# A table of PSUM banks in the lru part, mod_b tiles one place later, and the attention reciprocal in two halves

## The chip, the cores and the metric
The kernel runs on one core of a Trainium2 chip. The metric is the device time of one execution in microseconds (us); before the change three runs gave 1354.24, 1352.58 and 1350.67 us, so the median is 1352.58 us.

## What is computed
Two transformer-like blocks on one sequence of 512 tokens with 1024 channels, all in fp32. Cut to what matters:

```python
# first block
p = modulate(rms(x), shift1, scale1) @ w_in          # q, kv, k_pe, f, ga, gb
q, k, v = mla(p); attn = softmax(q k^T) v            # 8 heads, 512 + 256 keys
x = x + g1 * ((sigmoid(ga)*(attn@w_o) + sigmoid(gb)*(fft2(f)@w_f)) @ w_out)
x = x + g2 * expert_choice(modulate(rms(x), shift2, scale2))    # 16 experts
# second block
z = rms(x) @ w_in_2                                  # lru_x, lru_gate, sc_b, sc_c, sc_x
u = causal_conv4(lru_x)
h = linear_recurrence(u, gates r and i of u)         # y_lru = h * gelu(lru_gate)
y_sc = sc_b * causal_conv3(sc_c * sc_x)
x = x + concat(y_lru, y_sc) @ w_out_2
x = x + (gelu(conv3(h2@w_g)) * conv3(h2@w_u)) @ w_down
return rms(x)
```

The vectors shift1, scale1, g1, shift2, scale2, g2 are the modulation: `silu(c) @ w_mod + b_mod`.

## The kernel before
**Products.** Activations lie with channels on the partitions, so a tile is 128 channels by 512 tokens and fills one PSUM bank. A weight block is 128x128. Each fp32 product is made from three fp32r ones (`mm3`, L958 to L960): high part by high part, high by low, low by high. A projection of 1024 channels takes 8 blocks of three matmuls, 24 in all, for one tile (`project`).

**Weights.** SyncE loads chunks of 1 MB (16 blocks) into a ring of four raw buffers. ScalarE copies each to the high part (`w_hi`, L1702) and GpSimd subtracts it for the low part (`w_lo`, L892), into rings of three. ScalarE does so in its own program order, once the chunk that had the place is used up (`SPLIT_DUE`).

**Order and banks.** `make_plan` lists every PSUM tile in TensorE's order, gives each a bank (by a table, or round robin over the banks of a `phase`), and notes which semaphore frees it. `open_tile` (on TensorE) waits until the tile that had the bank before is freed. Nobody else decides the order: every engine has one program written out by hand, and what stands behind a waiting instruction waits with it.

**mod_b.** The last two thirds of the modulation are not done by TensorE's array but by VectorE: `modulation_b(c)` multiplies and adds eight slices of a raw chunk (L2108, L2110) and leaves a column sum `macc`; TensorE only adds its partitions (`mod_b_tile`, L995: four matmuls of one column), and VectorE reads the result (`mod_b_evac`, L2095). There are 16 of these. TensorE has them behind the tiles of ga, gb and four_o: number 0 stands behind ga tile 3, number 5+j behind gb tile j, number 12+j behind four_o tile j for j = 1 to 3. VectorE gets to `modulation_b(0)` only when it is done with the q rows (`q_rows`, L2292 the add of the rotated part). Number c+4 is made behind the evacuation of number c, and the raw chunks of weights stand in the same ring behind those of mod_b.

**Attention.** For each head h, TensorE makes six score tiles (`sT`), with the maxima of the next head between them (`max_pair`, L1237), then `pv` (L1271), the transposed maxima, and the transposes of q and k of head h+2. On VectorE, each head is: `head_lo(h+1)`, three ops (L2354) that give the low parts of q and k of the next head and so free banks 5, 3 and 4 for its score maxima; `maxima(h+1)` (L2363); `head_output(h-1)` (L2373, one operand in PSUM). In every even head from 2 on, `pair_output` follows: the reciprocal of the pair's sums `rs` (L2380, 128x512) and the product `att*rs` (L2381, both operands in SBUF). GpSimd adds up the probabilities of each head (`add_probs`, L915) and, after heads 1, 3 and 5, makes one `w_lo` (L892).

**lru part.** TensorE makes the eight lru_x tiles, behind them pairs of small gate tiles (lru_r, lru_i, L1535 and L1538) from the convolved channels `conv_u` (VectorE, L2626 to L2637, `lru_conv`), then for four groups sc_c, sc_x, sc_b, then eight lru_gate tiles, then mix_o (`w_out_2`; the first two tiles together, block by block, over four y_sc and eight y_lru parts). An lru_x tile is freed by `conv_done`, lru_r by ScalarE, lru_i by `lru_b_done` (VectorE, L2642), lru_gate by the low part of y_lru (L2073). The first two lru_x tiles have banks 3 and 4; from the third on banks go round robin over eight in the order 0, 1, 2, 5, 6, 7, 3, 4, and so to the end of lru_gate. By this, lru_x 5 has the bank of lru_x 3, lru_gate 6 and 7 have banks 0 and 1, and mix_o has

```python
bank=(0, 1, 2, 3, 4, 5, 4, 5)[j]
```

so that mix_o 0 and 1 take the banks of lru_gate 6 and 7.

Of the kernel before, what the change touches and what calls it, by code (L numbers as in the profile page):

```python
# [19 lines left out]
H = 8  # L20
# [13 lines left out]
LRU = 8  # L34
# [16 lines left out]
B = 128  # L51
# [4 lines left out]
FH = T // 2  # L56
# [19 lines left out]
def q_block(half, k):  # L76

    i = half * QL + k
    return S1_Q + i // 5 * CH + i % 5 * QW
# [123 lines left out]
def blocks(base, first, count, width=B):  # L203

    return range(base + first // CH, base + (first + count * width - 1) // CH + 1)


def split_steps():

    o = Order()  # L210
    for j in range(KD):
        o.add("h", j)
    for j in range(KD):
        o.add("hc", j)
    o.add("f", 0)
    o.add("f", 1)
    for j in range(QL):
        o.add("cq", j)
    for j in range(KL):
        o.add("ckv", j)  # L220
    o.add("f", 2)
    o.add("f", 3)
    for g in range(NF + 1):
        if g < NF:
            o.add("f_ch", g, 0)
            o.add("f_ch", g, 1)
        if g >= 1:
            o.add("four", g - 1)
    for h in range(H):
        o.add("q", h)  # L230
        o.add("k", h, 0)
        o.add("k", h, 1)
    for j in range(4):
        o.add("attn", j)
    for j in range(KD):
        o.add("m", j)
    for i in range(PAIRS):
        o.add("ye", i, 0)
        o.add("ye", i, 1)
    for j in range(KD):  # L240
        o.add("g", j)
    for j in range(SC):
        o.add("y_sc", j)
    for j in range(LRU):
        o.add("y_lru", j)
    for j in range(KD):
        o.add("g2", j)
    for q in range(QUARTERS):
        for i in range(FQ):
            o.add("ff", q, i)  # L250
    return o


SPLITS = split_steps()
# [7 lines left out]
PRE_FF = PRE_SC + SC + LRU  # L262
GATES_AFTER = {3: (0,), 4: (1, 2), 5: (3,), 6: (4,), 7: (5,)}
GATES_LAST = (6, 7)


SQ0 = 5 + QL + KL + 1
# [10 lines left out]
def make_plan():  # L278
    p = Plan()
# [37 lines left out]
    for half in range(2):  # L317
        for t in range(TT):
            p.add("uq", half, t, by=("qtok_done", half * TT + t + 1), bank=half * TT + t,
                  split=[c for k in range(QL) for c in blocks(s1, q_block(half, k), 1, QW)])  # L320
    p.phase(6)
    for j in range(KD):
        p.add("ga", j, by="act", split=blocks(s1, S1_GA + j * 8 * B, 8))
        if j >= 3:
            p.add("mod_b", j - 3, by=("modb_done", j - 2))
    for j in range(KD):
        p.add("gb", j, by="act", split=blocks(s1, S1_GB + j * 8 * B, 8))
        p.add("mod_b", 5 + j, by=("modb_done", 6 + j))

    def four_o(j, bank=None):  # L330
        p.add("four_o", j, by=("resid_done", j + 1), split=blocks(s1, S1_FO[j], NF), bank=bank)

    for j in range(KD // 2):
        four_o(j)
        if j >= 1:
            p.add("mod_b", 12 + j, by=("modb_done", 13 + j))
    for t in range(KT):
        p.add("uk", t, by=("ktok_done", t + 1), split=blocks(s1, S1_K, 8), bank=t)
    for t in range(KT):
# [80 lines left out]
    w = SPLIT0["w_in_2"]  # L420

    def lru_gates(i):
        p.add("lru_r", i, by="act")
        p.add("lru_i", i, by=("lru_b_done", i + 1))

    for j in range(LRU):
        if j == 2:
            p.phase(8, (0, 1, 2, 5, 6, 7, 3, 4))
        p.add("lru_x", j, by=("conv_done", j + 1), split=blocks(w, j * 8 * B, 8), bank=3 + j if j < 2 else None)
        for i in GATES_AFTER.get(j, ()):  # L430
            lru_gates(i)
    for j in range(SC):
        p.add("sc_c", j, split=blocks(w, (LRU + 3 * j) * 8 * B, 8))
        if j == 0:
            for i in GATES_LAST:
                lru_gates(i)
        p.add("sc_x", j, split=blocks(w, (LRU + 3 * j + 1) * 8 * B, 8))
        p.add("sc_b", j, by=("lo_done", SPLITS["y_sc", j] + 1), split=blocks(w, (LRU + 3 * j + 2) * 8 * B, 8))
    for j in range(LRU):
        p.add("lru_gate", j, by=("lo_done", SPLITS["y_lru", j] + 1), split=blocks(w, (LRU + 3 * SC + j) * 8 * B, 8))  # L440
    for j in range(KD):
        p.add("mix_o", j, by=("resid_done", RES2 + j + 1), split=blocks(SPLIT0["w_out_2"], j * 12 * B, 12),
              bank=(0, 1, 2, 3, 4, 5, 4, 5)[j])
    w = SPLIT0["ffn"]
    p.phase(5)
    for q in range(QUARTERS):
# [6 lines left out]


PLAN = make_plan()
TILE = PLAN.tiles
LAST = PLAN.last_user
# [28 lines left out]
def build(nc, stream, cols_d, x_d, ctx_d, router_d, wab_d, rope_d, rope_t_d, rot_d, dftc_d, ident_d, iota_d, xt_d, out):  # L486
    with ExitStack() as ctx:
        base = 16512

        def at(name, kb, shape, dt=F32):  # L490
            return nc.alloc_sbuf_tensor_at(name, shape, dt, offset=base + int(kb * 1024))

        def sem(name):
            return ctx.enter_context(nc.semaphore(name))
# [91 lines left out]
        rs = at("rs", R + 98, [P, T])  # L586
# [57 lines left out]
        sc_c = at("sc_c", R + 112, [P, T])  # L644
# [33 lines left out]
        freed_act = sem("freed_act")  # L678
        freed_dve = sem("freed_dve")
        hi_done = sem("hi_done")  # L680
        lo_done = sem("lo_done")
# [5 lines left out]
        modb_done = sem("modb_done")  # L687
# [48 lines left out]
        conv_done = sem("conv_done")  # L736
        a_sq_done = sem("a_sq_done")
        lru_b_done = sem("lru_b_done")
# [189 lines left out]
        def _(pe):  # L928
# [3 lines left out]
            def open_tile(*name):  # L932

                t = TILE[name]
                prev = PLAN.prev[t]
                if prev is not None:
                    pe.wait_ge(freeing[PLAN.freed[prev][0]], PLAN.freed_count(prev))
                return psum[:, PLAN.bank[t], :]
# [51 lines left out]
            def mod_b_tile(k):  # L990

                o = open_tile("mod_b", k)
                pe.wait_ge(macc_done, k + 1)
                for m in range(2):
                    last = mm(o[:, m:m + 1], macc[:, k % 4, m, :], one, start=True, stop=True)  # L995
                done(last)
# [182 lines left out]

            for j in range(KD):  # L1180
                done(project(open_tile("ga", j), s1, S1_GA + j * 8 * B, B, ks, hx))
                if j >= 3:
                    mod_b_tile(j - 3)
            for j in range(KD):
                done(project(open_tile("gb", j), s1, S1_GB + j * 8 * B, B, ks, hx))
                mod_b_tile(5 + j)
            pe.wait_ge(lo_done, SPLITS["four", NF - 1] + 1)

            def four_out(j, behind=None):
# [8 lines left out]

            for j in range(KD // 2):
                four_out(j)  # L1200
                if j >= 1:
                    mod_b_tile(12 + j)

            def token_rows(o, t, off):
                tok = slice(t * P, t * P + P)
# [365 lines left out]
            for j in range(SC):  # L1571
                for i, name in enumerate(("sc_c", "sc_x", "sc_b")):
                    done(project(open_tile(name, j), w2, (LRU + 3 * j + i) * 8 * B, B, ks, bx))
                    if i == 0 and j == 0:
                        for g in GATES_LAST:
                            gates(g)
# [108 lines left out]
        def _(act):  # L1685
# [313 lines left out]
            for j in range(SC):  # L1999
                split_weights(TILE["sc_c", j])  # L2000
                if j == 0:
                    for i in GATES_LAST:
                        lru_gates(i)
# [54 lines left out]
        def _(dve):  # L2058
            V = nc.vector
            n = [0]  # L2060

            def link(ins):

                n[0] += 1
                ins.then_inc(dve_seq, 1)
                dve.wait_ge(dve_seq, n[0])
# [26 lines left out]
            def mod_b_evac(k):  # L2093
                m = 16 + 2 * k
                V.tensor_tensor(mod[:, m:m + 2, 0], take("mod_b", k)[:, 0:2], col("b_mod", m, 2), ALU.add)\  # L2095
                    .then_inc(modb_done, 1)
# [89 lines left out]
            sums = [0]  # L2186
# [19 lines left out]
            for s in range(2):  # L2206
                w = slice(0, T) if s == 0 else slice(T, TK)
# [48 lines left out]
            for i in range(2):  # L2256
                w = rope_t[:, i * TT:(i + 1) * TT, :]
# [45 lines left out]
            for c in range(5):  # L2303
                mod_b_evac(c)
                modulation_b(c + 4)
            for c in range(5, 13):
                mod_b_evac(c)
                if c + 4 < 16:
                    modulation_b(c + 4)
# [6 lines left out]

            for j in range(KD // 2):
                four_gate(j)
                if j >= 1:
                    mod_b_evac(12 + j)  # L2320

            V.memset(k_hi[0][QK:QK + 1, :].bitcast(F32), 1.0)
            V.memset(k_lo[0][QK:QK + 1, :].bitcast(F32), 0.0)
# [45 lines left out]
            def head_output(h):  # L2369

                dve.wait_ge(o_raw, h + 1)
                r0 = (h % 2) * VD
                V.tensor_tensor(att[r0:r0 + VD, h // 2, :], psum[r0:r0 + VD, 6 + h % 2, :], att[r0:r0 + VD, h // 2, :],  # L2373
                                ALU.add).then_inc(o_sum, 1)

            def pair_output(j):

                dve.wait_ge(freed_act, PLAN.freed_count(TILE["sums", j]))
                dve.wait_ge(o_sum, 2 * j + 2)
                link(V.reciprocal(rs[:], rs[:]))  # L2380
                V.tensor_tensor(att[:, j, :], att[:, j, :], rs[:], ALU.mult).then_inc(att_done, 1)  # L2381

            def gate_behind(q):
# [10 lines left out]
            for h in range(H):  # L2394
                if h + 1 < H:
                    head_lo(h + 1)
                    maxima(h + 1)
                if h >= 1:
                    head_output(h - 1)
                if h >= 2 and h % 2 == 0:  # L2400
                    pair_output(h // 2 - 1)
            for j in range(3):
                lo(att_lo[:, j, :], att[:, j, :], att_hi[:, j, :], "attn", j).then_inc(lo_done, 1)
            head_output(H - 1)
            pair_output(H // 2 - 1)


# [169 lines left out]
            for i in range(PAIRS):  # L2577
# [24 lines left out]
                for half in range(2):  # L2602
# [5 lines left out]
                    w = slice(half * T, half * T + T)  # L2608
# [93 lines left out]
            for q in range(QUARTERS):  # L2702
                for i in range(FQ + 1):
                    if i < FQ:
# [14 lines left out]
                        if g >= 2:  # L2719
                            p = SPLITS["ff", (g - 2) // FQ, (g - 2) % FQ]  # L2720
# [14 lines left out]
            for n in range(1, len(Y_TILES), 2):  # L2735
                half, t = Y_TILES[n]
# [157 lines left out]
```

## Time and profile before

| what | value |
| --- | --- |
| median of 3 runs | 1352.58 us |
| the profiled execution, its own time | 1351.49 us |
| its span on the core | 1349.6 us |
| TensorE busy | 1319.4 us, 98% |
| VectorE busy | 691.6 us, 51% |
| ScalarE busy | 461.7 us, 34% |
| GpSimd busy | 433.2 us, 32% |
| granted TensorE clock, mean | 0.991 of full speed |

The span is the time from the first to the last instruction of the core; the execution's own time is 1.9 us longer. All rows have times from the span's start. In a timeline a row gives start, busy time, engine, line, operation, output and inputs with their shapes, a count, and in brackets the idle time of the engine just before and what ended it. The ends of matmuls overlap, so TensorE's pace is read from one start to the next.

### The profile page before, as it was taken

How to read it: one execution, taken by the hardware profiler on the slowest of the kernel's cores; microseconds unless marked ns; L12 is line 12 of the kernel's file. 1: busy time of each engine (PE TensorE's matmuls, PEld its weight loads, DVE VectorE, ACT ScalarE, POOL GpSimd, SP SyncE). 2: the span in 40 equal slices, each digit the busy share in tenths (PEclk: the TensorE clock that was granted, in tenths of full speed). 3: DMA queues.
4: the chain of work that ended last, by engine and by line, in shares of the span. 5: the costliest groups of instructions: out<-in, count | busy, mean ns of one | idle time of the engine just before them, and what ended most of it. 6: DMA issues, size and time to landing. Idle time of an engine off the chain costs nothing.

```text
span 1349.6 us, 15820 instructions
## 1 busy us (share of the span) xinstructions
PE 1319.4 (98%) x6366; PEld 970.1 (72%) x6366; DVE 691.6 (51%) x1261; ACT 461.7 (34%) x618; POOL 433.2 (32%) x136
## 2 busy tenths in 40 slices
PE   8999999999999899999999999899999999999998
PEld 5689788865578734444356788688888888888887
DVE  2465987567783723333257656512463451551553
ACT  4334222346631211121144571423342341431431
POOL 3144244237712000000024343524254345344440
PEclk9999999999999899999999999999999999999999
DMA  9521297301025899999973122223132222223101
GB/s 373 212 94 63 77 346 296 122 1 63 32 94 187 297 381 420 421 420 421 421 318 125 63 93 95 94 72 107 69 115 105 95 94 95 92 93 125 63 1 63
DMA packets 34501, 226.70 MB, mean 168 GB/s; under 512 B 4064, under 2 KB 4704, under 8 KB 8448
## 3 DMA queue, kind: packets, MB, share of 16 engines
q1 hardware_dynamic: 32992, 218.93, 42.3%
q0 software_dynamic: 1152, 4.19, 0.8%
q10 hardware_dynamic: 288, 2.62, 0.5%
q8 instruction: 48, 0.79, 0.2%
q14 instruction: 21, 0.17, 0.0%
HBM read 221.53 MB, written 4.19 MB: 167 GB/s over the span
## 4 chain that ended last, share of the span: by engine, by line
PE 91%; DVE 5%; ACT 1%; issue 1%; DMA 1%; POOL 0%; SPq 0%; DVEq 0%; ACTq 0%
PE psum L958 23%; PE psum L960 22%; PE psum L959 22%; PE psum L1463 12%; PE psum L1271 1%; PE psum L1237 1%; PE psum L1448 1%; PE psum L1451 1%; DVE q_tok L2292 1%; DMA x<-in_x 1%; PE psum L1423 1%; PE psum L1005 1%; PE psum L1672 1%; DVE rs L2380 0%; PE psum L1010 0%
## 5 line engine op out<-in xcount | busy, mean ns | idle before, releaser
L892 POOL TENSOR_TENSOR w_lo<-raw,w_hi 128x2048 fp32r<-128x2048 f32 x79 | 364.9, 4621 | 606.7 <-ACT w_hi L1702 606.7
L958 PE MATMUL psum<-b_hi,w_hi 128*128 128x512 f32 x608 | 238.7, 393 | 2.7 <-DVE conv_u L2637 2.5
L959 PE MATMUL psum<-b_lo,w_hi 128*128 128x512 f32 x608 | 237.3, 390 | 0.0
L960 PE MATMUL psum<-b_hi,w_lo 128*128 128x512 f32 x608 | 237.3, 390 | 0.0
L1702 ACT ACTIVATE w_hi<-raw 128x2048 fp32r<-128x2048 f32 x80 | 152.5, 1907 | 138.4 <-PE psum L960 105.6
L958 PEld LDWEIGHTS psum<-b_hi,w_hi 128*128 128x128 f32 x608 | 114.6, 188 | 33.6 <-issue 4.9
L960 PEld LDWEIGHTS psum<-b_hi,w_lo 128*128 128x128 f32 x608 | 114.6, 188 | 23.9
L959 PEld LDWEIGHTS psum<-b_lo,w_hi 128*128 128x128 f32 x608 | 114.4, 188 | 23.4
L1463 PE MATMUL psum<-ex_ring,xe 128*64 128x512 f32 x488 | 108.8, 595 | 0.9 <-ACT xe L1927 0.9
L2428 DVE TENSOR_TENSOR x<-psum,x 128x512 f32<-128x512 f32 x40 | 27.5, 691 | 132.2 <-PE psum L960 132.1
L958 PE MATMUL psum<-h_hi,w_hi 128*128 128x512 f32 (+1 forms) x208 | 85.2, 410 | 1.3 <-POOL w_lo L875 1.3
L960 PE MATMUL psum<-h_hi,w_lo 128*128 128x512 f32 (+1 forms) x208 | 82.7, 398 | 0.0
L959 PE MATMUL psum<-h_lo,w_hi 128*128 128x512 f32 (+1 forms) x208 | 82.4, 396 | 0.0
L1463 PEld LDWEIGHTS psum<-ex_ring,xe 128*64 128x64 f32 x488 | 34.1, 137 | 66.3 <-issue 65.4
L958 PE MATMUL psum<-ff_hi,w_hi 128*128 128x512 f32 x192 | 74.7, 389 | 0.0
L959 PE MATMUL psum<-ff_lo,w_hi 128*128 128x512 f32 x192 | 74.7, 389 | 0.0
L960 PE MATMUL psum<-ff_hi,w_lo 128*128 128x512 f32 x192 | 74.7, 389 | 0.0
L2709 DVE TENSOR_TENSOR psum<-psum,rstd_s 128x512 f32<-128x512 f32 x48 | 33.5, 697 | 77.4 <-PE psum L960 77.4
L902 POOL DMA_INDIRECT xg<-xt,ids x8 | 8.2, 1031 | 189.6 <-DVE ids L2538 138.8
L2430 DVE SCALAR_TENSOR_TENSOR x<-psum,mod,x 128x512 f32<-128x512 f32 x72 | 51.0, 743 | 25.7 <-PE psum L960 21.0
L1927 ACT ACTIVATE xe<-psum,mod,small 128x128 f32<-128x128 f32 x64 | 23.8, 458 | 83.6 <-PE psum L1423 83.6
L1463 PE MATMUL psum<-ex_ring,act_e 128*64 128x512 f32 x224 | 49.7, 595 | 0.7 <-DVE act_e L2596 0.7
(419 smaller groups left out, 2296.6 us busy)
## 6 DMA issues: line engine op xcount, KB each, us to landing
raw<-in_stream SPq DMA_DIRECT2D x97, 1024.0 KB, 4.9
ex_ring<-in_stream SPq DMA_DIRECT2D x89, 1024.0 KB, 17.3
mod_in<-in_stream SPq DMA_DIRECT2D x8, 1024.0 KB, 20.9
ex_last<-in_stream SPq DMA_DIRECT2D x7, 1024.0 KB, 17.0
x<-in_x SPq DMA_DIRECT2D x4, 512.0 KB, 6.9
x<-in_x ACTq DMA_DIRECT2D x1, 2048.0 KB, 7.4
xt<-h2t SPq DMA_DIRECT2D x8, 256.0 KB, 11.7
out<-y_out SPq DMA_DIRECT2D x8, 256.0 KB, 3.3
```

The costliest lines, as they stand in the source:

```text
L892: nc.gpsimd.tensor_tensor(w_lo[:, slot, :], raw[:, raw_slot, :], w_hi[:, slot, :].bitcast(F32), ALU.subtract).then_inc(w_lo_done, 1)
L958: mm(o, w[0], x[0], start=start, stop=False)
L959: mm(o, w[0], x[1], start=False, stop=False)
L960: return mm(o, w[1], x[0], start=False, stop=stop)
L1005: mm(psum[:, bank, 0:P], ones[:], ones[:], start=True, stop=True)
L1237: done(mm(o[:, 0:KH], q_hi[b][0:QK, q * P:(q + 1) * P], k_hi[b][0:QK, s * KH:(s + 1) * KH], start=True, stop=True))
L1463: last = mm(o[e * CAP:(e + 1) * CAP, :], x_of(k, e), w[:, (2 * (k - k0) + e) * T:(2 * (k - k0) + e + 1) * T], start=k == 0, stop=k == ks - 1)
L1702: A(w_hi[:, c % NHL, :], raw[:, n % NRAW, :], ACT.Copy).then_inc(w_hi_done, 1)
L1927: ins = A(xe[:, i % 2, k, :], o[:, j * P:(j + 1) * P], ACT.Identity, bias=mod[:, 3 * KD + k, 0:1], scale=a2[:, k:k + 1])
L2428: ins = V.tensor_tensor(x1[:, j, :], o, x1[:, j, :], ALU.add)
L2430: ins = V.scalar_tensor_tensor(out=x1[:, j, :], in0=o, scalar=scale, in1=x1[:, j, :], op0=ALU.mult, op1=ALU.add)
L2709: V.tensor_tensor(o, o, rstd, ALU.mult).then_inc(ffz_done, 1)
```

## The change
It has three parts.

**1. mod_b.** TensorE makes mod_b tile 0 behind ga tile 4 and not behind ga tile 3, and every later one is one place later too: 4+j behind gb tile j, 12+j behind four_o tile j, now from j = 0. VectorE's evacuation of tile 12 moves behind the gate of four_o 0. The round robin over six banks of this phase shifts with them.

**2. Banks of the lru part.** Tables give the banks of lru_x, lru_r and lru_i. sc_c, sc_x and sc_b of group 0 get banks 4, 5, 6; from sc_c 1 on there is a round robin over six banks. mix_o gets another table.

**3. Reciprocal.** `pair_output` no longer makes it. A new function `sums_inverse(j, half)` takes the reciprocal of one half of the 512 columns; half 0 stands at the end of the even head, half 1 at the end of the odd head after it, and `pair_output` (now only the product) behind half 1. For the last pair both halves come one after the other.

```diff
+X_BANKS = (3, 4, 0, 1, 6, 0, 1, 6)
+R_BANKS = (2, 2, 3, 2, 2, 2, 2, 3)
+I_BANKS = (5, 7, 4, 3, 5, 7, 0, 1)
...
-        if j >= 3:
-            p.add("mod_b", j - 3, by=("modb_done", j - 2))
+        if j >= 4:
+            p.add("mod_b", j - 4, by=("modb_done", j - 3))
...
-        p.add("mod_b", 5 + j, by=("modb_done", 6 + j))
+        p.add("mod_b", 4 + j, by=("modb_done", 5 + j))
...
     for j in range(KD // 2):
         four_o(j)
-        if j >= 1:
-            p.add("mod_b", 12 + j, by=("modb_done", 13 + j))
+        p.add("mod_b", 12 + j, by=("modb_done", 13 + j))
...
     def lru_gates(i):
-        p.add("lru_r", i, by="act")
-        p.add("lru_i", i, by=("lru_b_done", i + 1))
+        p.add("lru_r", i, by="act", bank=R_BANKS[i])
+        p.add("lru_i", i, by=("lru_b_done", i + 1), bank=I_BANKS[i])
 
     for j in range(LRU):
-        if j == 2:
-            p.phase(8, (0, 1, 2, 5, 6, 7, 3, 4))
-        p.add("lru_x", j, ..., bank=3 + j if j < 2 else None)
+        p.add("lru_x", j, ..., bank=X_BANKS[j])
...
     for j in range(SC):
-        p.add("sc_c", j, ...)
+        if j == 1:
+            p.phase(6, (2, 0, 3, 1, 4, 5))
+        p.add("sc_c", j, ..., bank=4 if j == 0 else None)
...
-        p.add("sc_x", j, ...)
-        p.add("sc_b", j, ...)
+        p.add("sc_x", j, ..., bank=5 if j == 0 else None)
+        p.add("sc_b", j, ..., bank=6 if j == 0 else None)
...
-              bank=(0, 1, 2, 3, 4, 5, 4, 5)[j])
+              bank=(5, 2, 0, 3, 1, 4, 1, 4)[j])
...
             for j in range(KD // 2):
                 four_out(j)
-                if j >= 1:
-                    mod_b_tile(12 + j)
+                mod_b_tile(12 + j)
...
+            def sums_inverse(j, half):
+
+                if half == 0:
+                    dve.wait_ge(freed_act, PLAN.freed_count(TILE["sums", j]))
+                w = slice(half * FH, half * FH + FH)
+                link(V.reciprocal(rs[:, w], rs[:, w]))
+
             def pair_output(j):
 
-                dve.wait_ge(freed_act, PLAN.freed_count(TILE["sums", j]))
                 dve.wait_ge(o_sum, 2 * j + 2)
-                link(V.reciprocal(rs[:], rs[:]))
                 V.tensor_tensor(att[:, j, :], att[:, j, :], rs[:], ALU.mult).then_inc(att_done, 1)
...
                 if h >= 2 and h % 2 == 0:
+                    sums_inverse(h // 2 - 1, 0)
+                if h >= 3 and h % 2 == 1:
+                    sums_inverse(h // 2 - 1, 1)
                     pair_output(h // 2 - 1)
             for j in range(3):
                 lo(att_lo[:, j, :], att[:, j, :], att_hi[:, j, :], "attn", j).then_inc(lo_done, 1)
             head_output(H - 1)
+            for half in range(2):
+                sums_inverse(H // 2 - 1, half)
             pair_output(H // 2 - 1)
```

## Rows read from the trace of the kernel before

**Rows 1.** The page's first part: busy time, share of span, instructions.
```profile
PE 1319.4 (98%) x6366; PEld 970.1 (72%) x6366; DVE 691.6 (51%) x1261; ACT 461.7 (34%) x618; POOL 433.2 (32%) x136
```

**Rows 2.** TensorE's waits: who for whom, us in total, times, longest.
```profile
PE psum L958 <- DVE ylru_lo L2073: 4.8, 1, 4.8
PE psum L995 <- DVE macc L2110: 3.0, 1, 3.0
PE psum L958 <- DVE conv_u L2637: 2.5, 1, 2.5
...
PE psum L1237 <- DVE k_lo L2354: 1.3, 2, 0.7
```

**Rows 3.** Timeline of TensorE around the wait for macc.
```profile
163.47 0.58 PE L995 MATMUL psum<-ones,macc 128*128 128x1 f32 x4 [2.95 <-DVE macc L2110]
...
168.56 0.39 PE L959 MATMUL psum<-h_lo,w_hi 128*128 128x512 f32 x1
...
171.08 0.50 PE L995 MATMUL psum<-ones,macc 128*128 128x1 f32 x4
```

**Rows 4.** Stretches: TensorE busy (x), weight loads busy (x), clock, DMA share, GB/s.
```profile
166.00:168.00 2.00, 2.00 (x6) 0.50 1.04 426
464.00:466.00 2.00, 2.00 (x11) 0.50 0.00 0
```

**Rows 5.** Timeline of TensorE, lru part, around the wait for conv_u.
```profile
734.86 0.60 PE L958 MATMUL psum<-b_hi,w_hi 128*128 128x512 f32 x1 [2.50 <-DVE conv_u L2637]
...
738.61 0.39 PE L958 MATMUL psum<-b_hi,w_hi 128*128 128x512 f32 x1
```

**Rows 6.** Timeline of TensorE, the first mix_o products.
```profile
872.53 0.76 PE L958 MATMUL psum<-ysc_hi,w_hi 128*128 128x512 f32 x1 [4.75 <-DVE ylru_lo L2073]
...
878.57 0.40 PE L960 MATMUL psum<-ysc_hi,w_lo 128*128 128x512 f32 x1
```

**Rows 7.** Timeline of GpSimd: the low part of weight chunk 11.
```profile
176.68 4.61 POOL L892 TENSOR_TENSOR w_lo<-raw,w_hi 128x2048 fp32r<-128x2048 f32 x1 [19.88 <-ACT w_hi L1702]
```

**Rows 8.** Timeline of VectorE: low part of y_lru 0, then that of y_lru 7.
```profile
849.97 0.69 DVE L2073 TENSOR_TENSOR ylru_lo<-psum,ylru_hi 128x512 fp32r<-128x512 f32 x1 [0.66 <-ACT ylru_hi L1712]
...
871.73 0.69 DVE L2073 TENSOR_TENSOR ylru_lo<-psum,ylru_hi 128x512 fp32r<-128x512 f32 x1 [0.66 <-ACT ylru_hi L1712]
```

**Rows 9.** Timeline of TensorE, heads 1 to 3: pv (L1271), first maxima (L1237).
```profile
300.77 1.94 PE L1271 MATMUL psum<-probs,v 128*64 128x512 f32 x8
...
308.19 0.62 PE L1237 MATMUL psum<-k_hi,q_hi 96*128 96x384 f32 x2
...
312.55 1.94 PE L1271 MATMUL psum<-probs,v 128*64 128x512 f32 x8
...
319.84 0.84 PE L1237 MATMUL psum<-k_hi,q_hi 96*128 96x384 f32 x2 [0.66 <-DVE k_lo L2354]
...
324.21 1.94 PE L1271 MATMUL psum<-probs,v 128*64 128x512 f32 x8
```

**Rows 10.** Timeline of VectorE, heads 2 to 4.
```profile
314.26 3.35 DVE L2380 RECIPROCAL rs<-rs 128x512 f32<-128x512 f32 x1
...
318.38 0.75 DVE L2354 SCALAR_TENSOR_TENSOR q_lo<-psum,cols,q_hi 96x512 fp32r<-96x512 f32 x1
...
325.15 0.67 DVE L2373 TENSOR_TENSOR att<-psum,att 64x512 f32<-64x512 f32 x1
328.04 0.75 DVE L2354 SCALAR_TENSOR_TENSOR q_lo<-psum,cols,q_hi 96x512 fp32r<-96x512 f32 x1 [2.21 <-ACT q_hi L1712]
```

**Rows 11.** Timeline of GpSimd: low part of a weight chunk, end of head 3.
```profile
326.84 4.58 POOL L892 TENSOR_TENSOR w_lo<-raw,w_hi 128x2048 fp32r<-128x2048 f32 x1
```

**Rows 12.** Timelines of GpSimd and VectorE, same stretch, in the attn_o stage.
```profile
389.49 4.65 POOL L892 TENSOR_TENSOR w_lo<-raw,w_hi 128x2048 fp32r<-128x2048 f32 x1 [18.63 <-ACT w_hi L1702]
...
390.50 4.19 DVE L2420 TENSOR_TENSOR m_tmp<-m_tmp,gbf 128x512 f32<-128x512 f32 x1
```

**Rows 13.** Timeline of TensorE: the shorter wait before the experts.
```profile
459.98 0.42 PE L1398 MATMUL psum<-ident,work 16*128 16x16 f32 x4 [1.78 <-DVE work L2511]
```

More of the change, by code:

```diff
@@ L422, in lru_gates @@
     def lru_gates(i):
-        p.add("lru_r", i, by="act")
-        p.add("lru_i", i, by=("lru_b_done", i + 1))
+        p.add("lru_r", i, by="act", bank=R_BANKS[i])
+        p.add("lru_i", i, by=("lru_b_done", i + 1), bank=I_BANKS[i])
     for j in range(LRU):
-        if j == 2:
-            p.phase(8, (0, 1, 2, 5, 6, 7, 3, 4))
-        p.add("lru_x", j, by=("conv_done", j + 1), split=blocks(w, j * 8 * B, 8), bank=3 + j if j < 2 else None)
+        p.add("lru_x", j, by=("conv_done", j + 1), split=blocks(w, j * 8 * B, 8), bank=X_BANKS[j])
         for i in GATES_AFTER.get(j, ()):
@@ L432, in make_plan @@
     for j in range(SC):
-        p.add("sc_c", j, split=blocks(w, (LRU + 3 * j) * 8 * B, 8))
+        if j == 1:
+            p.phase(6, (2, 0, 3, 1, 4, 5))
+        p.add("sc_c", j, split=blocks(w, (LRU + 3 * j) * 8 * B, 8), bank=4 if j == 0 else None)
         if j == 0:
@@ L436, in make_plan @@
                 lru_gates(i)
-        p.add("sc_x", j, split=blocks(w, (LRU + 3 * j + 1) * 8 * B, 8))
-        p.add("sc_b", j, by=("lo_done", SPLITS["y_sc", j] + 1), split=blocks(w, (LRU + 3 * j + 2) * 8 * B, 8))
+        p.add("sc_x", j, split=blocks(w, (LRU + 3 * j + 1) * 8 * B, 8), bank=5 if j == 0 else None)
+        p.add("sc_b", j, by=("lo_done", SPLITS["y_sc", j] + 1), split=blocks(w, (LRU + 3 * j + 2) * 8 * B, 8),
+              bank=6 if j == 0 else None)
     for j in range(LRU):
@@ L1181, in _ @@
                 done(project(open_tile("ga", j), s1, S1_GA + j * 8 * B, B, ks, hx))
-                if j >= 3:
-                    mod_b_tile(j - 3)
+                if j >= 4:
+                    mod_b_tile(j - 4)
             for j in range(KD):
                 done(project(open_tile("gb", j), s1, S1_GB + j * 8 * B, B, ks, hx))
-                mod_b_tile(5 + j)
+                mod_b_tile(4 + j)
             pe.wait_ge(lo_done, SPLITS["four", NF - 1] + 1)
@@ L2305, in _ @@
                 modulation_b(c + 4)
-            for c in range(5, 13):
+            for c in range(5, 12):
                 mod_b_evac(c)
@@ L2318, in _ @@
                 four_gate(j)
-                if j >= 1:
-                    mod_b_evac(12 + j)
+                mod_b_evac(12 + j)
             V.memset(k_hi[0][QK:QK + 1, :].bitcast(F32), 1.0)
```

## Prediction, made before the changed kernel was run
> **What bounds the kernel now.** I read the page's busy times first. TensorE is busy for 98% of the span, the others for about half or less [rows 1]: a change can gain only where TensorE stands still or runs slowly. So the list of TensorE's waits comes next. Its three largest entries are 4.8, 3.0 and 2.5 us, once each, and one of 1.3 us in two pieces comes from the attention [rows 2]. Third, the timeline around each: when TensorE resumes, its matmuls start 0.43 us apart for a while and not 0.23, and the granted clock of such a stretch is 0.50, that is 1.2 and not 2.4 GHz [rows 4]. A wait of 2.5 us or more thus costs more than itself. The pace at full clock is (171.08 - 168.56) / 11 = 0.229 us per matmul [rows 3].
>
> **Part 1, mod_b.** The same 16 tiles are made, the same DVE work is done; only TensorE's place for them moves. Before, TensorE is at tile 0 at 163.47 - 2.95 = 160.5 and waits until the column sum is there [rows 3]. With another ga tile first it gets there at 160.5 + 24 x 0.229 = 166.0, 2.5 us after the sum. The wait of 2.95 goes. From 163.47 to 171.08 lie one mod_b tile (some 0.4) and 24 matmuls (5.5): 7.6 where 5.9 is the full pace, so 1.7 of slow clock goes too. **Gain 4.65 us.** What is late next: weight chunk 11 hangs on mod_b chunks that VectorE frees, not on TensorE, so it doesn't come earlier. Its low part is done at 176.68 + 4.61 = 181.3 [rows 7]. TensorE wants it behind the 15th matmul of ga tile 7: 160.5, three whole tiles (5.5 each), three mod_b tiles (0.4 each) and 15 x 0.229 come to 181.6. The margin is 0.3 us. I count nothing, and up to 1 us for the range. After that VectorE makes a sum in 8 ops of about 0.5 us, 4.1 in all, and TensorE wants one per 5.9 us; the wait list has no second wait at L995 [rows 2]. VectorE's evacuations stand at most one place behind, where it has slack. Round robin over six banks leaves the same six tiles between users: nothing.
>
> **Part 2, banks of the lru part.** No instruction is added. lru_x 5 had the bank of lru_x 3 and waited for that tile's convolution. Now it has the bank of lru_x 2, whose convolution is one turn of VectorE (some 4 us) earlier, so the wait of 2.50 goes. The nine matmuls from 734.86 to 738.61 took 3.75, at full pace 2.06 [rows 5]: 1.7 more. **Gain 4.2 us.** lru_x 6 now needs lru_x 3 and lru_x 7 needs lru_x 4, both convolved before TensorE is there; gate tiles of ScalarE alternate on banks 2 and 3 with a whole tile between them.
>
> At the end, mix_o 0 and 1 are opened together, and mix_o 1 had the bank of lru_gate 7. So not one of their 72 matmuls could start before y_lru 7, although that is needed only as the last of twelve parts. With banks 5 and 2 they follow lru_gate 2 and 3. The wait of 4.75 goes. From 872.53 to 878.57 lie 14 matmuls: 6.04, at full pace 3.21, so 2.8 more [rows 6]. **Gain 7.6 us.** Next late is y_lru 7 itself, done at 871.73 + 0.69 = 872.4 [rows 8]; TensorE wants it 66 matmuls after 867.8, at 882.9. Margin 10 us. The six-bank round makes lru_gate 6 wait for y_lru 0, done at 849.97 + 0.69 = 850.7 [rows 8]; TensorE wants the bank two tiles before its stop at 867.8, at 856.8. Margin 6 us. VectorE, ScalarE and GpSimd are driven by TensorE's tiles there, so all of this moves forward together with the 4.2 us.
>
> **Part 3, the reciprocal.** Its cost in columns is the same: 3.35 us for 512 [rows 10], so I estimate 1.7 for each half.
>
> Good side: in head 2 the reciprocal and the product stand before head_lo(4). It starts at 318.38, and the first maxima 1.46 later, 0.66 late [rows 9, 10]. With half a reciprocal and no product VectorE is free 2.4 us earlier, which is more than the 0.66. The same in head 4 to 5. **Gain 1.3 us**, the whole entry of the wait list [rows 2].
>
> Bad side: heads 3 and 5 now end with the other half and the product. GpSimd makes a low part of weights there, from 2.6 us after the start of that head's pv (324.21, 326.84) to 7.2 after it [rows 9, 11]. VectorE's head_output starts 0.9 after pv (325.15), takes 0.7, the half takes 1.7: the product `att*rs` wants to start 3.3 after pv, inside GpSimd's op. It has two SBUF operands. No such product meets GpSimd in the trace of before, but `m_tmp*gbf`'s addition, the same form and size, does: it took 4.19 instead of 0.69, ending 0.55 after GpSimd's op that had begun 1 us before it [rows 12]. By that row the product ends at 7.2 + 0.55 = 7.75 after pv. head_lo then starts, and the first maxima 1.46 later, at 9.2. TensorE wants them 308.19 - 300.77 = 7.4 after pv [rows 9]. **Loss 1.8 us each in heads 4 and 6, 3.6 in all.** The bounds of it: nothing if the product isn't held up (it would end 4.0 after pv, when the q of the next head is only just ready: it starts at 3.8 [rows 9, 10]), and 3.6 + 3.4 if each stop also brings the slow clock at 1.7 a time [rows 3, 5]. The nearest row for the clock is a wait of 1.78 after which it did drop [rows 13, 4], but thin products stand on either side of that one, and here full ones; I take none.
> The rule behind it is in the Trainium skill, "SBUF — State Buffer", section "Who interferes with whom": a VectorE instruction with two inputs in SBUF and a GpSimd instruction that reads SBUF exclude each other, and the later one waits for the whole of the earlier one. It speaks against the place of the product, and rows 12 agree with it. By it the sum of the attention is a loss of 2.3; without it a gain of 1.3.
>
> Last pair: the two halves one after the other cost some 0.1 more than one whole, and the product of pair 2 stands before them. att_lo 3 comes about 0.8 later; TensorE first has 36 matmuls of attn_o with the other three parts (8.2 us) over the old chain of about 6. Covered; if not, up to 1 us.
>
> **Sum.** 4.65 + 4.2 + 7.6 + 1.3 - 3.6 = 14.15 us. Against the profiled execution that is 1351.49 - 14.15 = 1337.3; it lies 1.1 under the median of the runs, and on the median the sum gives 1338.4. I say **1338.2 us**.
>
> **Rivals.**
> (a) The product isn't held up: GpSimd's op comes later than I think, or the form behaves otherwise. For it: this line never overlapped. Against: rows 12. Gain 17.75, time 1334.8. Chance 0.20.
> (b) The held-up product also costs the clock, in both heads. For it: rows 13. Time 1338.4 + 3.4 = 1341.8. Chance 0.15.
> (c) The lru part keeps only one of its two gains: a new owner of a bank, or a part of y_lru, is late where one stood before. Against: margins of 6 and 10 us. Without the 7.6 it is 1346.0. Chance 0.05. That the bank table doesn't do what it says (the wait at the first mix_o products stays) is the same case.
> (d) Slower: the clock, once down in heads 4 and 6, stays down while the attention's short matmuls run. After the wait before the experts it was still at 0.50 some 4 us later [rows 13, 4]. A head is 11.7 us at full clock [rows 9]; all four heads from 4 to 7 at half clock would cost up to 47 us, and it decides from 14.15 + 4.1 = 18 us, about a head and a half wholly at half clock. Against: after longer waits full pace came back within 3.8 to 6.1 us [rows 5, 6]. At one and three quarters of a head it loses 20.5 and gives 1358.9. Chance 0.03.
>
> **The numbers.** Forecast 0.57. A time counts as the same within 0.3%, about 4 us, which is what this measurement can tell. The forecast, (a), (b) and (c) all lie below 1348.5: faster 0.95. Same 0.02, for (c) with further losses. Slower 0.03. Range: (a) with 1.8 for the spread of the runs gives 1333.0; (b) with 0.7 for chunk 11 and the last pair gives 1342.5. That leaves out (c), (d) and tails.
>
> **What would show it.** TensorE's wait list without ylru_lo, macc and conv_u, and full clock around ga tile 4, lru_x 5 and the first mix_o products: parts 1 and 2. In the attention: no wait for k_lo in heads 3 and 5, but two of about 1.8 us in heads 4 and 6; the product L2381 with two of four ops near 4 us and L2380 with eight of 1.7. If the two waits are absent, (a) holds. If the first mix_o products still wait, or lru_gate 6 does, part 2 is wrong; if chunk 11's `w_lo` shows as a wait of over 1 us, part 1 is.

## The result, and the profile after

The kernel after took 1339.14 us (median of 4 runs, 1338.94 to 1340.03), the kernel before on the same chip 1351.97 us: ratio 0.9905, 95% interval [0.9887, 0.9922], 12.8 us less. The forecast was 1338.2. All medians are those of the undisturbed executions; one execution of the experiment e3 below, at 2648.91 us twice as long as the others, is left out. The profiled execution of after took 1340.03 us with a span of 1338.1, so in the two traces the gain is 11.5 us where the sum had said 14.15.

First the page's busy times and TensorE's waits of the kernel after, to be laid beside [rows 1, 2]. Its line numbers are 2 to 11 higher than before.

```profile
PE 1317.2 (98%) x6366; PEld 969.1 (72%) x6366; DVE 696.6 (52%) x1265; ACT 461.6 (34%) x618; POOL 433.5 (32%) x136
```

```profile
PE psum L1284 <- DVE q_lo L2355: 3.5, 2, 1.8
...
PE psum L1400 <- DVE work L2522: 1.6, 1, 1.6
```

The waits for ylru_lo, macc, conv_u and k_lo are gone, as forecast. One entry of two times 1.8 us is new, and stands at L1284: that is the matmul which adds up a pair's probabilities (the sums tile), and not the first maxima.

To see where the 11.5 us come from, both traces are cut at the same instructions. The first line ends where TensorE would want tile 0 of mod_b at its old place: that is ahead of its wait (163.47 - 2.95) in before, and one ga tile (24 x 0.229 = 5.50) ahead of the tile in after.

| stretch | before, us | after, us | gain | forecast |
| --- | --- | --- | --- | --- |
| start to mod_b 0 wanted | 160.52 | 160.09 | 0.4 | 0 |
| to the first copy of v (ScalarE) | 98.60 | 94.04 | 4.6 | 4.65 |
| to the first attn_o product: attention | 113.76 | 117.55 | -3.8 | -2.3 |
| to the first expert product | 99.63 | 101.05 | -1.4 | 0 |
| to the first mix_o product | 400.02 | 391.25 | 8.8 | 4.2 + 4.75 |
| to the first y_lru product (24 matmuls on) | 8.32 | 5.44 | 2.9 | 2.8 |
| to the end | 468.7 | 468.7 | 0.0 | 0 |

**Parts 1 and 2.** TensorE's timelines of the kernel after, in the order of [rows 3, 5, 6]: no wait stands before any of the three places, and 12 products of mix_o (863.98 to 866.70, 2.72 us) run at the full pace of 0.227.

```profile
165.59 0.50 PE L998 MATMUL psum<-ones,macc 128*128 128x1 f32 x4
...
171.53 0.50 PE L998 MATMUL psum<-ones,macc 128*128 128x1 f32 x4
...
732.85 0.50 PE L961 MATMUL psum<-b_hi,w_hi 128*128 128x512 f32 x1
...
863.98 0.39 PE L961 MATMUL psum<-ysc_hi,w_hi 128*128 128x512 f32 x1
```

The low parts that I had called next late are in time. VectorE's timeline of after, y_lru 0 and 7, as in [rows 8]: the last is done at 868.79, and TensorE wants it 66 matmuls after 863.98, at 879.1. GpSimd's low part of chunk 11 began at 175.84, 0.84 earlier than in [rows 7], and no wait followed.

```profile
846.37 0.69 DVE L2075 TENSOR_TENSOR ylru_lo<-psum,ylru_hi 128x512 fp32r<-128x512 f32 x1 [0.67 <-ACT ylru_hi L1714]
...
868.10 0.69 DVE L2075 TENSOR_TENSOR ylru_lo<-psum,ylru_hi 128x512 fp32r<-128x512 f32 x1 [0.66 <-ACT ylru_hi L1714]
```

**Part 3.** VectorE's timeline of after at the end of head 3, then GpSimd's and TensorE's of the same stretch:

```profile
319.28 0.67 DVE L2374 TENSOR_TENSOR att<-psum,att 64x512 f32<-64x512 f32 x1
319.88 1.73 DVE L2382 RECIPROCAL rs<-rs 128x256 f32<-128x256 f32 x1
321.65 4.51 DVE L2387 TENSOR_TENSOR att<-att,rs 128x512 f32<-128x512 f32 x1
326.08 0.73 DVE L2355 SCALAR_TENSOR_TENSOR q_lo<-psum,cols,q_hi 96x512 fp32r<-96x512 f32 x1
```

```profile
319.81 1.27 POOL L918 TENSOR_TENSOR psum_odd<-psum_odd,probs 128x512 f32<-128x512 f32 x1 [0.49 <-ACT probs L1862]
321.03 4.58 POOL L895 TENSOR_TENSOR w_lo<-raw,w_hi 128x2048 fp32r<-128x2048 f32 x1
```

```profile
318.48 1.94 PE L1273 MATMUL psum<-probs,v 128*64 128x512 f32 x8
...
326.87 0.64 PE L1284 MATMUL psum<-psum_even,ones 128*64 128x512 f32 x1 [1.77 <-DVE q_lo L2355]
```

GpSimd's op ends at 321.03 + 4.58 = 325.61, the product at 326.16: 0.55 later, to the hundredth what [rows 12] had shown for another product. The forecast had its end 7.75 after pv; it is 7.68. The low part of q comes behind it and frees the bank of the sums tile, which TensorE wanted at 326.87 - 1.77 = 325.1. The half of the reciprocal ahead of it, which reads one operand in SBUF, also began behind a GpSimd op (319.88 behind 319.81, `add_probs`), and took the 1.73 that a half takes elsewhere. At the end of head 5 VectorE's rows come again:

```profile
344.55 1.73 DVE L2382 RECIPROCAL rs<-rs 128x256 f32<-128x256 f32 x1
346.32 4.54 DVE L2387 TENSOR_TENSOR att<-att,rs 128x512 f32<-128x512 f32 x1
350.78 0.74 DVE L2355 SCALAR_TENSOR_TENSOR q_lo<-psum,cols,q_hi 96x512 fp32r<-96x512 f32 x1
```

Last, the stretches of the kernel after (TensorE busy, loads busy, granted clock, DMA share and GB/s) at two places where the clock fell and had not before: behind the second wait in the attention, and ahead of the experts.

```profile
354.00:356.00 2.00, 2.00 (x7) 0.50 0.26 107
...
442.00:444.00 2.00, 2.00 (x12) 0.50 0.97 406
```

### The profile page after: what moved, and what is told of

It is laid out like the page before. It is cut to its first block, busy times and chain, and to the rows that moved or that the text cites. A ratio compares the mean times of both kernels' runs of the same rounds, so it can differ in the third digit from the quotient of the medians.

```text
span 1338.1 us, 15827 instructions
## 1 busy us (share of the span) xinstructions
PE 1317.2 (98%) x6366; PEld 969.1 (72%) x6366; DVE 696.6 (52%) x1265; ACT 461.6 (34%) x618; POOL 433.5 (32%) x136
## 4 chain that ended last, share of the span: by engine, by line
PE 93%; DVE 3%; DMA 3%; ACT 1%; issue 0%; POOL 0%; SPq 0%; DVEq 0%; ACTq 0%
PE psum L961 24%; PE psum L962 23%; PE psum L963 23%; PE psum L1465 11%; DMA ex_last<-in_stream 2%; PE psum L1273 1%; PE psum L1239 1%; PE psum L1450 1%; PE psum L1453 1%; DVE att L2387 1%; DMA x<-in_x 1%; PE psum L1008 1%; PE psum L1537 1%; PE psum L1425 1%; PE psum L1674 1%; PE psum L1013 0%
```

## The experiments

Each run below but e9, which is a single execution, is a median of 4 to 12 executions, timed against the kernel before; edits are to the kernel after where nothing else is said. To set the kernels side by side beyond the spread of single runs I cut every trace at the same instructions as in the table above. The attention is the stretch from the first copy of v to the first attn_o product, the router that from there to the first expert product:

| kernel | attention, us | router, us | falls of the clock in the attention |
| --- | --- | --- | --- |
| before | 113.76 | 99.63 | none |
| after, three profiles | 117.55, 117.53, 117.57 | 101.05, 100.66, 101.04 | one each |
| e4, e5 | 117.64, 117.57 | 99.69, 99.09 | one each |
| e6, e10 | 116.32, 116.31 | 99.65, 99.15 | none |
| e3 | 116.26 | 99.69 | none |
| e7 (before with part 3) | 116.33 | 99.72 | none |
| e2 | 114.12 | 99.80 | none |
| e1, e12 | 112.35, 112.33 | 98.91, 99.47 | none |

**GpSimd held behind the product (e1).** The product must not meet `w_lo`, at the cost of a later `w_lo`.

```diff
+                if SPLIT0["wo"] + 1 <= c <= SPLIT0["wo"] + 2:
+                    pool.wait_ge(att_done, c - SPLIT0["wo"])
                 if c == LAST_SPLIT:
                     gather_tokens()
                 lo(c, c % NHL)
```

> The changed kernel, but GpSimd's low part of the weight chunk at the ends of heads 3 and 5 waits until VectorE has made the product att*rs. Theory (the product is held up by GpSimd's op because both read two SBUF operands): both L2387 ops fall from 4.5 to 0.7 us, TensorE's two waits of 1.77 us at the sums vanish, and the slow clock in head 6 (1.2 us) with them: some 4.8 us faster than the changed kernel, 1334.4 us. Rival (VectorE simply has too much to do in the odd heads, GpSimd doesn't matter): the product stays at 4.5 us or what follows it is as late as before, time unchanged at 1339.1. Second rival (GpSimd, begun 0.9 us later, is late for the sums of the next head): the wait at the sums stays but is released by GpSimd.

Measured: 1334.14 us, ratio 0.9872 [0.9855, 0.9888]. VectorE's timeline of this kernel, then GpSimd's:

```profile
321.49 1.74 DVE L2384 RECIPROCAL rs<-rs 128x256 f32<-128x256 f32 x1
323.26 0.69 DVE L2389 TENSOR_TENSOR att<-att,rs 128x512 f32<-128x512 f32 x1
323.94 0.75 DVE L2357 SCALAR_TENSOR_TENSOR q_lo<-psum,cols,q_hi 96x512 fp32r<-96x512 f32 x1
```

```profile
324.03 4.58 POOL L895 TENSOR_TENSOR w_lo<-raw,w_hi 128x2048 fp32r<-128x2048 f32 x1 [1.32 <-DVE att L2389]
```

The product takes 0.69 us and GpSimd's op still 4.58, now one behind the other: the 3.8 us were held-up time, and nothing else was changed. The new wait keeps GpSimd idle for 1.32 us, and TensorE's waits for `w_lo` are no longer than in before (1.3 us in all). Both waits at the sums are gone and the attention takes 1.41 us less than before, where I had 1.3 for the good side of part 3. This shows that the overlap with GpSimd's op costs the time. That it does so because of the two SBUF operands was not tried by an edit; it rests on the rule cited in the prediction and on the reciprocal half above, which ran beside `add_probs` unhindered. No kernel here had a lower median.

**Everything at the end of even heads (e2).** Both halves and the product stand where they stood before; only the split in two remains.

```diff
-                    sums_inverse(h // 2 - 1, 0)
-                if h >= 3 and h % 2 == 1:
-                    sums_inverse(h // 2 - 1, 1)
+                    for half in range(2):
+                        sums_inverse(h // 2 - 1, half)
                     pair_output(h // 2 - 1)
```

> The changed kernel, but both halves of the reciprocal and the product stand at the end of the even head, as one stood before the change. Theory: k_lo is late again in heads 3 and 5 (0.7 us each, the waits of before) and the two waits of 1.77 us and the slow clock in head 6 vanish: 3.7 us of loss in the attention go, so 1335.4 us. Rival (the reciprocal's place costs nothing, the rest of the change made the attention slower): no change, 1339.1.

Measured: 1335.32 us, ratio 0.9876 [0.9858, 0.9894], as expected (1335.4). TensorE's waits of this kernel have the old entry again, a little longer than in [rows 2], since two halves take 0.1 more than one whole:

```profile
PE psum L1239 <- DVE k_lo L2355: 1.5, 2, 0.8
```

The attention takes 114.12, so 0.36 more than before and 3.4 less than the profiled run of after: the place of the second half and of the product is what costs.

**The places of mod_b undone (e3).** TensorE has tile 0 behind ga tile 3 again, and all others one place earlier; bank order and evacuations with them.

```diff
-            p.add("mod_b", j - 4, by=("modb_done", j - 3))
+            p.add("mod_b", j - 3, by=("modb_done", j - 2))
...
-                    mod_b_tile(j - 4)
+                    mod_b_tile(j - 3)
```

> The changed kernel with the mod_b tiles at their old places, the rest as changed. Theory: a wait of about 2.9 us at mod_b 0 and 1.7 us of slow clock behind it come back: 4.65 to 5.0 us slower than the changed kernel, 1343.8 to 1344.1 us. Rival (the place of mod_b matters little because weight chunk 11 bounds the stage anyway): under 1 us slower.

Measured: 1344.0 us (five executions, 1341.83 to 1346.77), ratio 0.9951 [0.9933, 0.9968], 4.5 above the median of all ten executions of after (1339.5). Its waits and its timeline at the place:

```profile
PE psum L999 <- DVE macc L2114: 3.0, 1, 3.0
```

```profile
163.97 0.58 PE L999 MATMUL psum<-ones,macc 128*128 128x1 f32 x4 [2.95 <-DVE macc L2114]
```

From this row to the first copy of v are 95.66 us, in before 95.65. From the same tile in after, and in four profiles that have it at the same place (e1, e9, e10, e11), they are 88.54 or 88.55. 95.66 + 2.95 - 88.55 - 5.50 = 4.56: the term of part 1 is confirmed, by the traces and by the medians.

**The banks of mix_o (e4) and of lru_x 5 (e5).** mix_o 0 and 1 follow lru_gate 6 and 7 again; lru_x 5 has the bank of lru_x 3 again.

```diff
-              bank=(5, 2, 0, 3, 1, 4, 1, 4)[j])
+              bank=(1, 4, 0, 3, 5, 2, 5, 2)[j])
```

> The changed kernel, but the first two mix_o tiles take the banks of lru_gate 6 and 7 (table 1, 4, 0, 3, 5, 2, 5, 2). Theory: a wait of about 4.8 us for the low part of y_lru 7 comes back, with 2.8 us of slow clock behind it: 7.6 us slower, 1346.7 us. Rival (the mix_o tiles wait somewhere else anyway, and the gain came from the other tables): under 2 us slower.

```diff
-X_BANKS = (3, 4, 0, 1, 6, 0, 1, 6)
+X_BANKS = (3, 4, 0, 1, 6, 1, 0, 6)
```

> The kernel after, with one edit: lru_x 5 takes the bank of lru_x 3 again (as before the change), lru_x 6 that of lru_x 2. Theory (my terms are right one by one): the wait for conv_u of 2.5 us comes back and 1.7 us of slow clock behind it, so 1339.1 + 4.2 = 1343.3 us. Rival (VectorE's convolutions only move the wait elsewhere: the gates would have waited anyway): under 1 us more, 1339.1 to 1340.1. A middle value near 1341.6 would say that the wait comes without the clock.

Measured: 1347.29 us, ratio 0.997 [0.9952, 0.9988], and 1344.0 us, ratio 0.9947 [0.9934, 0.996]. TensorE's timeline of e4, then of e5:

```profile
869.09 0.75 PE L961 MATMUL psum<-ysc_hi,w_hi 128*128 128x512 f32 x1 [4.75 <-DVE ylru_lo L2075]
...
876.24 0.39 PE L961 MATMUL psum<-ylru_hi,w_hi 128*128 128x512 f32 x1
```

```profile
736.82 0.79 PE L961 MATMUL psum<-b_hi,w_hi 128*128 128x512 f32 x1 [2.50 <-DVE conv_u L2648]
...
740.44 0.40 PE L961 MATMUL psum<-b_hi,w_hi 128*128 128x512 f32 x1
```

Both waits return at their old length. In e5 nine matmuls take 3.62 us (in before 3.75), so 1.6 of slow clock: 4.1 in all where the sum had 4.2. In e4 the 24 matmuls take 7.15 us, after a wait as long as in before, where they took 8.32: the slow clock cost 1.7 here, not 2.9. The median of e4 is 7.8 above that of after, close to the 7.6 of the sum, but its trace shows only 6.5 at this place (4.75 and 1.7).

**Filler in place of the wait (e6, e10).** The banks of e4, and matmuls on constants ahead of mix_o, so that TensorE's array doesn't stand still.

```diff
+            idle_products(44, 7)
             project_two((open_tile("mix_o", 0), open_tile("mix_o", 1)),
```

> The banks of mix_o that make its first products wait for y_lru 7 (as in the run before with the wait of 4.75 us), but 44 matmuls of 128 columns on constants stand in front of them, which take 44 x 0.114 = 5.0 us by the row of 76 in 8.65 us: TensorE works on nothing of use in the time in which it stood still. Theory (the 2.8 us beyond the wait are slow clock, and the clock falls because the array stands still): no wait or a small one, full clock behind it, 1339.1 + 5.0 = 1344.1 us, 3.2 less than with the bare wait (1347.3). Rival (the slow clock comes from something else there, or filler doesn't hold it): still 0.50 behind it and 1347 to 1348 us.

Measured: 1348.29 us, ratio 0.9982 [0.9971, 0.9992], against the expected 1344.1: a miss, through my own count, and 0.3 from the time that I had given to the rival (1347 to 1348). One filler product is two matmuls in the trace, so they took twice as long; the clock behind them, which decides, was full. TensorE's timeline of e6:

```profile
862.01 9.98 PE L1008 MATMUL psum<-ones 128*128 128x128 f32 x88
871.75 0.48 PE L961 MATMUL psum<-ysc_hi,w_hi 128*128 128x512 f32 x1
```

With 21 in place of 44:

> As the filled run before, with 21 filler products and not 44: each is two matmuls in the trace (88 in 9.98 us), so 44 filled twice the time that they should. 21 x 2 x 0.1134 = 4.8 us, as long as the bare wait. Theory (slow clock comes only from the standing still): the start of the first mix_o products is as late as with the bare wait, the clock behind it full, so 1339.1 + 4.8 = 1343.9 us, 2.8 to 3.4 less than with the bare wait (1347.3). Rival (the slow clock isn't cured by filler of 128 columns, or only by the double amount): 1346.5 to 1347.5 and rows at 0.50 behind it.

Measured: 1342.18 us, ratio 0.993 [0.9916, 0.9944]. TensorE's timeline of e10, then the stretch behind it, with the clock at 1.00:

```profile
861.45 4.85 PE L1008 MATMUL psum<-ones 128*128 128x128 f32 x42
866.36 0.47 PE L961 MATMUL psum<-ysc_hi,w_hi 128*128 128x512 f32 x1
...
871.93 0.39 PE L961 MATMUL psum<-ylru_hi,w_hi 128*128 128x512 f32 x1
```

```profile
868.00:870.00 2.00, 2.00 (x10) 1.00 0.00 0
```

The filler holds mix_o back by 4.91 us, where the bare wait took 4.75, but the 24 matmuls take 5.57 us (5.54 in e6) where e4 and before had 7.15 and 8.32, and after 5.44. So the slow clock behind this wait comes from the array standing still, and its price stands beside the wait's own length. The whole run came out 2.4 us above after, not 4.8. The profiles of e10 and after differ by 1.2: the filler costs 4.9, but the attention is 1.2 us shorter and the stretch from there to the lru part 1.4, where the clock fell less in this execution, and the last stage is 1.3 shorter. In that stage TensorE's matmuls stand at the same times to 0.01 us, and what is shorter is the stretch behind VectorE's last op (3.25 us in e6 and in e10, 4.53 in after, 5.06 in e4). Why that is so in both filler kernels wasn't tried.

**Part 3 alone on the kernel before (e7).** The last two blocks of the change's diff, nothing else.

> The kernel before with part 3 alone: the reciprocal in two halves, the product at the end of the odd heads; mod_b and all banks as before. Against the kernel before (1351.2 on the chip of the earlier runs). Theory (the product is held up by GpSimd's w_lo): two waits of 1.8 us for q_lo at the sums, 2.3 us slower without a fall of the clock and 3.7 to 4 with one in head 6, so 1353.5 to 1355.2 us. Rival (the product isn't what costs; the loss seen after comes from how the parts meet): 1.3 us faster, 1349.9.

Measured: 1354.02 us (12 runs, 1350.74 to 1359.37), ratio 1.0022 [1.0009, 1.0034]: 2.4 us slower. Its waits have the new entry and the old three of [rows 2]:

```profile
PE psum L958 <- DVE ylru_lo L2073: 4.8, 1, 4.8
PE psum L1282 <- DVE q_lo L2354: 3.6, 2, 1.8
PE psum L995 <- DVE macc L2110: 3.0, 1, 3.0
PE psum L958 <- DVE conv_u L2647: 2.5, 1, 2.5
```

The attention takes 116.33, 2.57 more than before, with no fall of the clock. That is the forecast's loss of 2.3, seen alone. Behind the wait of 4.75 us the 24 matmuls take 8.43 us here (877.33 to 885.76), so 3.0 of slow clock, as in before.

**The kernel after again, for its clock (e9, one execution; e11, 5 rounds), and e1 again beside it (e12).**

> The kernel after once more, unchanged, for its clock: does TensorE's clock fall again in head 6 (352 to 356 us) and between 442 and 449 us, and nowhere else but between 462 and 469? If the falls belong to the kernel, at the same places, to within 2 us; if they belong to the execution, one or both are missing and the span is 1 to 3 us shorter than 1338.1.

> The kernel after, unchanged, timed beside the others: 1339.1 us was seen in one series and 1342.4 in a single execution of another. If the falls of the clock in heads 4 and 6 and ahead of the experts come and go by execution, single times spread over some 3 to 4 us (1338 to 1342) and the median lies near 1340; if they belong to the kernel, all lie within 1 us.

> The kernel after with GpSimd's w_lo held behind the product, once more, beside the kernel after on the same chip. Theory: 4.5 to 5.5 us less than the kernel after of this series (two waits of 1.8 and the falls of the clock that sometimes follow them), ratio to before near 0.987. Rival (its 1334.1 was a lucky series): under 3.5 us less, the two waits alone.

Measured: 1342.35 us; 1339.8 us (1338.69 to 1341.51), ratio 0.9906 [0.9893, 0.992]; 1334.23 us, ratio 0.9869 [0.9854, 0.9884]. So e1 repeats itself, 5.6 us below after; 5.2 of it lie in the attention (117.57 against 112.33). The five times of e11 spread over 2.8 us around 1339.8, which fits falls that come and go by execution, though the start of the kernel spreads as much (below). In e9 the falls did move, but the span is 1340.5 and not 1 to 3 us shorter than 1338.1, as I had tied to that: the start alone took 2.4 us longer. TensorE's timeline of the attention in e9, pv of heads 3 to 5 and the second wait:

```profile
320.89 1.94 PE L1273 MATMUL psum<-probs,v 128*64 128x512 f32 x8
...
329.29 0.64 PE L1284 MATMUL psum<-psum_even,ones 128*64 128x512 f32 x1 [1.76 <-DVE q_lo L2355]
335.83 1.94 PE L1273 MATMUL psum<-probs,v 128*64 128x512 f32 x8
...
346.75 1.94 PE L1273 MATMUL psum<-probs,v 128*64 128x512 f32 x8
...
355.15 0.64 PE L1284 MATMUL psum<-psum_even,ones 128*64 128x512 f32 x1 [1.76 <-DVE q_lo L2355]
```

Its stretches behind the first of these waits and behind the second:

```profile
332.00:334.00 2.00, 2.00 (x7) 0.50 0.07 29
...
356.00:358.00 2.00, 1.97 (x9) 1.00 0.97 410
```

Here the clock fell in head 4 and not in head 6; in the first profile of after it was the other way round, with waits equal to 0.01 us. Head 4 takes 335.83 - 320.89 = 14.94 us with a fall, 332.24 - 318.48 = 13.76 without (first profile), 11.79 in e1 without the wait. A wait costs 2.0, a fall 1.2 more. Seven profiles, the three of after among them, are of kernels that are the same up to the lru part; five of them have one fall in the attention, none has two. So the place of the fall belongs to the execution, and the attention took 117.5 to 117.6 us or 116.3 and nothing between.

## Why the prediction was right, and where its steps were off

**What bounds it.** Right: TensorE stayed at 98%, and the gain came from its own waits and its clock alone.

**Part 1, 4.65 us.** Right to 0.1 (4.56). Chunk 11 showed no wait. Thirteen traces also show that the start of the kernel, up to where mod_b 0 is wanted at its old place, varies by 3.3 us between executions (159.4 to 162.7); my range had 1.8 for all spread of the runs.

**Part 2, 4.2 and 7.6 us.** Right. From the lru_x 5 products to the first y_lru product before took 880.85 - 734.86 + 2.50 = 148.5 us, after 869.42 - 732.85 = 136.6: 11.9 against 11.8. What I took for a constant, the slow clock behind a wait of 4.75, is not one: 2.9 in before and 3.0 in e7, which are the same kernel in this part, but 1.7 in e4, which has other banks ahead of it. With one profile of each, whether the execution or the kernel sets it stays open.

**Part 3, good side 1.3 us.** Right: 1.41 in e1, where only it acts. In after heads 3 and 5 (pv to pv) take 10.91 and 10.94 us where before has 11.66 [rows 9] and 11.64, so 1.5 in all.

**Part 3, bad side 3.6 us.** The mechanism was right, and it was known before the run as an argument against this change: the product is held up by GpSimd's op. By the rule in the Trainium skill, "SBUF — State Buffer", section "Who interferes with whom", the later of two such instructions waits for the whole of the earlier one; the trace agrees in both cases (the product ends 0.55 us after GpSimd's op), and in e1, where the two don't overlap, VectorE's takes 0.69. Two things were wrong in it. **Who waits:** I wrote that head_lo starts late and the first maxima want it at 7.4 after pv. In fact the matmul of the sums (L1284) needs the bank that q_lo frees, and wants it at 325.1 - 318.48 = 6.6 after pv. It waits until 8.4, so the wait is 1.77 all the same: that 1.8 was right in size is luck, from two differences that cancel, an earlier want and an earlier release (q_lo alone, not the whole of head_lo and the maxima's start). **The step that failed is the next one**, "here full ones; I take none": the clock does fall behind such a wait, in one of the two heads, in 5 of 9 profiles with these waits, at 1.2 us. The loss per wait is also 2.0 and not 1.8 by the periods, so the attention lost 2.5 without a fall and 3.8 with one, against 2.3. The last pair was covered, as forecast: no wait for `att_lo` is in the list of after. Rival (b) had the fall in both heads at 1.7 each; no profile shows that.

**Not in the sum: 1.4 us in the router stage.** All three profiles of after have a fall of the clock between 440 and 451 us that before has not. Cut finer, from the column sums ahead of the router (L1013) to the transposes of `aff` (L1392), the thirteen profiles give 7.82 to 7.84 us in eight cases without a fall in that piece and 8.98 to 9.15 in five with one: 1.2 us, the same price as in the attention. The five are the three of after, e5 and e6. e1 and e10 have a fall too, but at the end of that piece or just behind it. In e5 and e6 the stage as a whole is no longer than before (99.09, 99.65), since TensorE then waited under 0.2 us for `work` (L1400), where before had 1.78 [rows 13] and the clock fell behind it; but in the next stage they wait 1.2 us more for expert weights (DMA). From the first attn_o product to the first lru_x product the eight take 323.0 to 323.5 us, the five 324.3 to 325.0. No edit stands in that stage, and e4 and e10, the same kernel as after up to there, are among the eight. Why all three profiles of after have this fall stays open.

**Rivals.** (a), a product not held up, was to give 1334.8; e1 made that happen by an edit and gave 1334.1 (without the clock's falls in the attention either), so its price was right and its premise false. (c) has nothing for it: both gains of part 2 came. (d), a clock that stays down, has nothing for it: each fall in the attention was over within 6 us of the wait ahead of it.

**The sum** was 14.15; the medians say 12.8 (13.0 in the later series) and the profiled pair 11.5. The two things missing from it, one fall in the attention (1.2, and 0.3 for the longer price of the waits) and one ahead of the experts (1.4), are small beside it, and other kernels with the same code there had executions without them. The profiled execution of after was the slowest of its four. That the forecast stands within 1 us of the median is in part luck: by the profiled pair it is 2.7 off.

## What to carry to other kernels

Before an operation with two SBUF operands is moved on VectorE, lay GpSimd's timeline beside its new place: here it went from 0.69 to 4.5 us twice, and one wait on GpSimd, which could spare 1.3 us, turned a part that cost 2.4 us into one that gains 1.4. Lay a table of PSUM banks against the times at which the tiles are wanted: here that was worth 12 us without one instruction less. Price a TensorE wait as itself plus a clock term: the clock fell behind each of the nine bare waits of 2.5 to 4.75 us in these profiles, for 1.6 to 3.0 us, and behind 5 of the 18 waits of 1.8 us in the attention, for 1.2. Compare kernels stage by stage between equal instructions: with the same number of falls, the attention repeated to 0.1 us where whole runs spread by 3.

## What the runs showed of the hardware that was not expected

- After two waits of the same length (1.76 to 1.79 us) between the same matmuls, the granted clock fell to 0.50 behind the first, behind the second or behind neither, never behind both: 5 falls in 9 profiles.
- The slow clock behind one and the same wait of 4.75 us cost 2.9 and 3.0 us in two profiles and 1.7 in a third. With matmuls on constants in its place (42 of 128 columns, 4.85 us) the clock stayed at 1.00, and the matmuls behind it took 0.1 us more than with no wait at all.
- A reciprocal of 128x256 takes 1.73 to 1.75 us on VectorE, half of that of 128x512 (3.35). It reads one operand in SBUF, and it wasn't held up where it began 0.07 us behind a GpSimd op with two (319.88 beside 319.81); the product with two operands, 0.62 behind another, was held for 3.8 us.
